# A two-layer decoder step: FFN statistics behind the last product, the mixer's sums and splits reordered, and samples finished on VectorE

## The reference, cut to what matters

```python
def layer(x, c, ...):
    mod = (silu(c) @ w_ada + b_ada).reshape(B, 9, D)
    s1, sc1, g1, s2, sc2, g2, s3, sc3, g3 = [mod[:, k] for k in range(9)]
    x = LN(ALPHA * x + 0.5 * (1 + g1) * swiglu(x * (1 + sc1) + s1), ln_g[0], ln_b[0])
    mix = mixer(x * (1 + sc2) + s2)          # pooling, RG-LRU, gate, @ w_out
    x = LN(ALPHA * x + (1 + g2) * mix, ln_g[1], ln_b[1])
    x = LN(ALPHA * x + 0.5 * (1 + g3) * swiglu(x * (1 + sc3) + s3), ln_g[2], ln_b[2])
```

## Time and profile before

| | |
|---|---|
| median of 3 runs | 998.52 us (998.02 to 999.37) |
| the profiled execution: its own time | 998.87 us |
| its span, first to last instruction | 997.1 us |
| mean granted TensorE clock | 0.997 |
| busy: PE, PEld | 978.1 us (98%), 932.2 us (93%) |
| busy: DVE, ACT, POOL | 611.8 us (61%), 450.6 us (45%), 103.6 us (10%) |
| PE product matmuls of lines 562 to 564 | x1648 each on `m`, x672 each on `h`; mean 283 to 287 ns |
| transfers | 235.67 MB, mean 236 GB/s |

### The profile page before, as it was taken

One profiled execution on the slowest core, in us unless ns is written; L12 is line 12 of the kernel. 1 busy time (PEld: TensorE's weight loads), 2 busy tenths in 40 slices (PEclk: granted clock), 3 DMA queues, 4 the chain that ended last, 5 costly groups with the idle time before them and its releaser, 6 DMA issues. The chain is left out here.

```text
span 997.1 us, 19778 instructions
## 1 busy us (share of the span) xinstructions
PE 978.1 (98%) x8598; PEld 932.2 (93%) x8598; DVE 611.8 (61%) x932; ACT 450.6 (45%) x546; POOL 103.6 (10%) x160
## 2 busy tenths in 40 slices
PE   6999999999999999999999999999999999999996
PEld 4999999998998999999989999999898899999996
DVE  2566454567898665554676655465689776555564
ACT  2354444235674545342345534343468554444340
POOL 1240000000310610000006000000030043000000
PEclk9999999999999999999999999999999999999998
DMA  9999888993749897959578796868563967664631
GB/s 335 321 253 334 275 260 297 317 333 122 295 138 306 289 261 196 313 181 318 181 229 240 196 326 189 298 212 295 170 244 106 330 168 212 190 188 154 227 112 44
DMA packets 259313, 235.67 MB, mean 236 GB/s; under 512 B 7647, under 2 KB 237145, under 8 KB 259210
## 3 DMA queue, kind: packets, MB, share of 16 engines
q1 hardware_dynamic: 256848, 230.71, 72.8%
q0 software_dynamic: 2080, 3.58, 1.2%
q10 hardware_dynamic: 298, 0.10, 0.0%
HBM read 233.11 MB, written 1.78 MB: 236 GB/s over the span
## 5 line engine op out<-in xcount | busy, mean ns | idle before, releaser
L562 PE MATMUL bank<-m_hi,w_hi 128*128 128x264 f32 x1648 | 470.7, 286 | 0.9 <-DVE m_lo L1206 0.5
L563 PE MATMUL bank<-m_lo,w_hi 128*128 128x264 f32 x1648 | 467.3, 284 | 0.0
L564 PE MATMUL bank<-m_hi,w_lo 128*128 128x264 f32 x1648 | 466.7, 283 | 0.0
L1134 DVE TENSOR_TENSOR w_lo<-raw,w_hi 128x2048 fp32r<-128x2048 f32 (+2 forms) x150 | 324.9, 2166 | 200.6 <-ACT w_hi L899 199.9
L899 ACT ACTIVATE w_hi<-raw 128x2048 fp32r<-128x2048 f32 (+2 forms) x149 | 266.8, 1792 | 173.9 <-PE bank L564 150.9
L562 PEld LDWEIGHTS bank<-m_hi,w_hi 128*128 128x128 f32 x1648 | 310.3, 188 | 7.8 <-issue 5.7
L563 PEld LDWEIGHTS bank<-m_lo,w_hi 128*128 128x128 f32 x1648 | 310.5, 188 | 0.1
L564 PEld LDWEIGHTS bank<-m_hi,w_lo 128*128 128x128 f32 x1648 | 309.3, 188 | 0.0
L562 PE MATMUL bank<-h_hi,w_hi 128*128 128x264 f32 x672 | 192.8, 287 | 0.0
L564 PE MATMUL bank<-h_hi,w_lo 128*128 128x264 f32 x672 | 190.9, 284 | 0.0
L563 PE MATMUL bank<-h_lo,w_hi 128*128 128x264 f32 x672 | 190.8, 284 | 0.0
(11 more groups left out here) (240 smaller groups left out, 560.3 us busy)
## 6 DMA issues: line engine op xcount, KB each, us to landing
raw<-in_ffn_wgu_dram SPq DMA_DIRECT2D x160, 512.0 KB, 5.2
ada_raw<-in_w_ada_dram SPq DMA_DIRECT2D x72, 1024.0 KB, 9.0
raw<-in_ffn_wdown_dram SPq DMA_DIRECT2D x48, 512.0 KB, 3.5
raw<-in_ffn_wdown_dram SPq DMA_DIRECT2D x48, 384.0 KB, 4.3
raw<-in_w_in_dram SPq DMA_DIRECT2D x24, 512.0 KB, 4.5
raw<-in_w_out_dram SPq DMA_DIRECT2D x16, 384.0 KB, 7.0
raw<-in_w_out_dram SPq DMA_DIRECT2D x8, 256.0 KB, 7.1
raw<-in_ffn_wgu_dram SPq DMA_DIRECT2D x2, 768.0 KB, 8.7
```

Source lines behind the costliest of these rows:

```text
L562: pe.matmul(out, hi, r_hi, start=start, stop=False)
L563: pe.matmul(out, hi, r_lo, start=False, stop=False)
L564: mm = pe.matmul(out, lo, r_hi, start=False, stop=stop)
L1134: dve.tensor_tensor(lo[:, 0:n], src[:, 0:n], hi[:, 0:n].bitcast(F32), ALU.subtract).then_inc(lo_split, 1)
```

## The change

- **FFN ends (three of the four).** The two statistics between output 6 and output 7 go. After output 7 PE sums `sqs[:, 0]`, `sqs[:, 6]`, `zsum`, `z[:, 7]`, `sqs[:, 7]`. `zsum` now holds tile 6 too: POOL adds it, in a new function `sum_seven`.
- **`variance`** multiplies the samples by their coefficient into `sq`, behind the first mean subtraction; `normalise` has one sample operation less there.
- **Mixer ends (both).** DVE takes tiles 2 to 5 one by one and adds each to `zsum`. PE sums `zsum`, tile 6 and tile 7. The coefficients come before the wait for the mean. The split of unit g0 + 6 comes after the mean's subtraction, ahead of `split_half` of g0 + 7; PE's wait for that half moves behind the first products.
- **Tail.** DVE does the samples' three steps and the transpose between the prompt's blocks; ACT stores one half of the samples and SP, behind the prompt's last block, the other.

```diff
+            def sum_seven(l, f):
+                n = l * 3 + 2 * f
+                pool.wait_ge(sums_ready, 2 * l + f + 1)
+                pool.wait_ge(evicted, n * DT + 7)
+                pool.tensor_tensor(zsum[:], zsum[:], z[:, 6], ALU.add).then_inc(seven_summed, 1)
...
             for l in range(DEPTH):
+                sum_seven(l, 0)
                 finish_x(l, 0)
...
                 if l + 1 < DEPTH:
+                    sum_seven(l, 1)
                     finish_x(l, 2)
...
-            samples = z[:, :, TP:T]
-            pool.wait_ge(samples_less_mean, 1)
-            pool.wait_ge(sample_rstd, 1)
-            pool.tensor_tensor(samples, samples, token_rstd[:, 2:2 + B].unsqueeze(1).broadcast_to([P, DT, B]), ALU.mult)\
...
                 for j in range(2):
+                    if f and j and k == 0:
+                        pe.wait_ge(half_split, l + 1)
...
                         for i in range(2):
-                            if pair == 3 and third == 2 and i == 1 and (l, f) != (DEPTH - 1, 1):
-                                pe.wait_ge(sums_ready, 2 * l + f + 1)
-                                stat(bank[MEAN], mean_w, zsum[:], True, False)
-                                stat(bank[VAR], mean_w, sqs[:, 0], True, False)
...
             def ffn_stats(l, f):
                 n, s = l * 3 + 2 * f, l * 15 + f * 10
-                pe.wait_ge(evicted, n * DT + 7)
-                stat(bank[MEAN], mean_w, z[:, 6], False, False)
+                pe.wait_ge(sums_ready, 2 * l + f + 1)
+                stat(bank[VAR], mean_w, sqs[:, 0], True, False)
                 pe.wait_ge(squared, s + 4)
                 stat(bank[VAR], mean_w, sqs[:, 6], False, False)
+                pe.wait_ge(seven_summed, 2 * l + f + 1)
+                stat(bank[MEAN], mean_w, zsum[:], True, False)
                 pe.wait_ge(evicted, n * DT + 8)
                 stat(bank[MEAN], mean_w, z[:, 7], False, True).then_inc(mean_out, 1)
...
             def mixer_stats(l):
                 n, s = l * 3 + 1, l * 15 + 5
-                pe.wait_ge(evicted, n * DT + 5)
+                pe.wait_ge(mixed_sum, l + 1)
                 stat(bank[MEAN], mean_w, zsum[:], True, False)
-                stat(bank[MEAN], mean_w, z[:, 4], False, False)
                 pe.wait_ge(evicted, n * DT + 7)
-                stat(bank[MEAN], mean_w, z[:, 5], False, False)
                 stat(bank[MEAN], mean_w, z[:, 6], False, False)
...
                 subtract_mean(0)
+                own.wait()
+                own.then(dve.tensor_tensor(sq[:, :, TP:T], z[:, :, TP:T], coef[:, 0, :, 1:C], ALU.mult))
...
-                split(g0 + 6)
-                residuals((2, 3))
-                dve.wait_ge(evicted, n * DT + 4)
-                for m in (2, 3):
-                    own.then(dve.tensor_tensor(zsum[:], zsum[:], z[:, m], ALU.add))
-                residuals((4,))
-                residuals((5, 6))
+                for m in range(2, 6):
+                    residuals((m,))
+                    dve.wait_ge(evicted, n * DT + m + 1)
+                    if m < 5:
+                        own.did(dve.tensor_tensor(zsum[:], zsum[:], z[:, m], ALU.add))
+                    else:
+                        dve.tensor_tensor(zsum[:], zsum[:], z[:, m], ALU.add).then_inc(mixed_sum, 1)
+                residuals((6,))
                 residuals((7,))
+                coefficients(l, 2)
                 dve.wait_ge(mean_out, n + 1)
                 dve.wait_ge(evicted, (n + 1) * DT)
                 for a, b in ((0, 1), (1, 2), (2, 4), (4, 6), (6, 8)):
                     dve.tensor_tensor(z[:, a:b], z[:, a:b], wide(bank[MEAN][:, 0:T], b - a), ALU.subtract)\
                        .then_inc(less_mean, b - a)
-                coefficients(l, 2)
+                split(g0 + 6)
                 split_half(g0 + 7, 0).then_inc(half_split, 1)
...
+            own.then(dve.tensor_tensor(samples, samples, weights, ALU.mult))
+            for i, (a, h) in enumerate(BLOCKS):
                 c = slice(h * HALF, (h + 1) * HALF)
                 dve.scalar_tensor_tensor(x_rows[:, a, c], x_rows[:, a, c], token_rstd[:, a:a + 1], bias_rows[:, c],
                                          ALU.mult, ALU.add).then_inc(y_ready, 1)
-            dve.wait_ge(sample_steps, 3)
-            dve.transpose(ys[:, 1], ys[:, 0]).then_inc(samples_turned, 1)
+                if i == 0:
+                    dve.wait_ge(sample_rstd, 1)
+                    own.did(dve.tensor_tensor(samples, samples, token_rstd[:, 2:2 + B].unsqueeze(1).broadcast_to([P, DT, B]),
+                                              ALU.mult))
+                elif i == 1:
+                    own.wait()
+                    own.did(dve.tensor_tensor(ys[:, 0].rearrange("p (b m) -> p m b", m=DT), samples, biases, ALU.add))
+                elif i == 2:
+                    own.wait()
+                    dve.transpose(ys[:, 1], ys[:, 0]).then_inc(samples_turned, 1)
```

More of the change, by code:

```diff
@@ L239, in trunk @@
         y_ready = sem("y_ready")
-        sample_steps = sem("sample_steps")
         consts = sem("consts")
@@ L314, in trunk @@
         trio_lo = sem("trio_lo")
+        mixed_sum = sem("mixed_sum")
+        seven_summed = sem("seven_summed")
         gu_view = [w.rearrange("l (k p) (h f c) -> l h f p k c", p=P, h=2, c=P) for w in (ffn1_wgu, ffn2_wgu)]
@@ L346, in trio_part, with store_samples @@
             return tile[:].rearrange("p s c -> p (s c)")[:, first + k0 * n:first + k1 * n]
+        def store_samples(eng, h):
+            eng.dma_start(y_sample[h * B // 2:(h + 1) * B // 2].rearrange("b o (m g j) -> g b (o m) j", g=4, j=32),
+                          ys[:, 1, 32 * h:32 * (h + 1)]).then_inc(y_stored, 16)
         block = ctx.enter_context(nc.Block())
@@ L422, in _ @@
                     .then_inc(y_stored, 16)
+            sync.wait_ge(samples_turned, 1)
+            store_samples(sync, 1)
             sync.wait_ge(y_stored, 6 * 16)
@@ L1111, in _ @@
             act.wait_ge(samples_turned, 1)
-            for h in range(2):
-                act.dma_start(y_sample[h * B // 2:(h + 1) * B // 2].rearrange("b o (m g j) -> g b (o m) j", g=4, j=32),
-                              ys[:, 1, 32 * h:32 * (h + 1)]).then_inc(y_stored, 16)
+            store_samples(act, 0)
         @block.vector
@@ L1261, in normalise @@
                 full(0)
-                own.then(dve.tensor_tensor(samples, z[:, :, TP:T], rstd[:, TP:T].unsqueeze(1).broadcast_to([P, DT, B]),
-                                           ALU.mult))
-                own.then(dve.tensor_tensor(samples, samples, coef[:, 0, :, 1:C], ALU.mult))
+                root = rstd[:, TP:T].unsqueeze(1).broadcast_to([P, DT, B])
+                if i == 1:
+                    own.then(dve.tensor_tensor(samples, z[:, :, TP:T], root, ALU.mult))
+                    own.then(dve.tensor_tensor(samples, samples, coef[:, 0, :, 1:C], ALU.mult))
+                else:
+                    own.then(dve.tensor_tensor(samples, samples, root, ALU.mult))
                 dve.tensor_tensor(samples, samples, coef[:, 1, :, 1:C], ALU.add).then_inc(sample_full, 1)
@@ L1623, in _ @@
             dve.wait_ge(mean_squared, 2 * DEPTH)
-            dve.tensor_tensor(z[:, :, TP:T], z[:, :, TP:T], bank[6][:, 0:B].unsqueeze(1).broadcast_to([P, DT, B]),
-                              ALU.subtract).then_inc(samples_less_mean, 1)
+            samples = z[:, :, TP:T]
+            weights, biases = (a.unsqueeze(2).broadcast_to([P, DT, B]) for a in (ln_g_of(DEPTH - 1, 2), ln_b_of(DEPTH - 1, 2)))
+            own.did(dve.tensor_tensor(samples, samples, bank[6][:, 0:B].unsqueeze(1).broadcast_to([P, DT, B]), ALU.subtract))
             dve.tensor_tensor(token_rstd[:, 2:2 + B], bank[7][:, 0:B], h_full[:, 0:B], ALU.subtract).then_inc(sample_var, 1)
```

3 lines of the change are left out of this document (removed).

## The result

The changed kernel takes 992.97 us (median of 6 runs, 992.31 to 994.17); the kernel before, in 6 runs beside them, 998.49 us (998.02 to 999.37). The medians are 5.5 us apart. The ratio is 0.995, with a 95% interval of 0.9939 to 0.9961, that is, 5.0 us faster, between 3.9 and 6.1. The forecast was 3.9 us, and the range began 0.7 us above what was measured. The profiled execution took 992.94 us with a span of 990.4, so the span is 6.6 us shorter. In the 36 runs of the changed kernel and of those built on it, it is 1.76 to 3.55, on average 2.41. So some 0.6 us of what the spans win doesn't reach the time. No part of the change shows this by itself, and no run shows what takes it.

The account below looks back on a forecast made before the run. PE was busy for 978.1 us, so time could be won by fewer matmuls, matmuls done during waits, or shorter waits. FFN ends 1.8, mixer ends 2.1 and tail 0 sum to 3.9 us: 998.52 to 994.6, range 993.7 to 996.8.

Parts of the forecast that it names:

- FFN end: Each of three FFN ends: 0.51 us from the last statistic coming sooner plus 0.08, together 0.59; 1.8 for three.
- the 0.08 is won too: FFN end: PE's wait of some 0.08 us for `m_lo`, ahead of the first product, goes.
- Mixer end: Each of two mixer ends: tile 7's statistic starts 1.07 us sooner; 2.1 for two.
- 1.33 a tile: Mixer end: DVE's time per tile in the new order, 0.59 + 0.21 + 0.44 + 0.09 us.
- DVE still binds: Mixer end: PE is done with tile 7 since 788.24, while DVE's last residual steps end at 789.92.
- The bound named for the mixer: Both mixer ends together: a gain from 0.1 to 2.3 us, with up to 1.0 lost if the split slid on.
- Splits behind the subtraction: Mixer end: splits of 2.2 and 1.1 us fit ahead of the first normalised tile, with 0.2 to spare.
- I take 0: Tail: last store done at 994.05 as before, so no gain; from -0.3 to +0.7 us.
- Nothing is left: Rival, chance 0.06: what comes sooner at the ends is waited for at a transfer later; 998.5 us.
- the two halves: Rivals: only the mixers gain, 996.4 us, chance 0.12; only the FFNs gain, 996.7 us, chance 0.10.
- POOL's longest row: Slower rival, chance 0.06: POOL's sum ends 2.06 us later, each FFN end loses about 1.5; 1000.8 us.
- The rule weighed: FFN end: GpSimd and two-SBUF-input VectorE operations exclude each other; tile 7's 8-column step would wait until 714.50.

Follow-up runs that it names:

- e9_sample_move: The kernel before with only the samples' coefficient multiplication moved into `variance`, behind the first mean subtraction; 1000.1 us in one run.
- e1_tail: The kernel before with the tail's part alone: samples on DVE between the blocks, stores split between ACT and SP; 997.3 us, ratio 0.9997.
- e4_pool_last: The whole change plus a one-column memset by POOL at the very end, which nothing waits for; 995.35 us, ratio 0.9971.
- e2_ffn: The kernel before with the FFN's part alone: two statistics moved, tile 6 summed by POOL, sample operation moved into `variance`; 997.6 us, ratio 0.9996.
- e3_mixer: The kernel before with the mixer's part alone: tiles summed one by one, three statistics instead of five, split behind the subtraction; 995.2 us, ratio 0.9971.
- e7_order_only: The kernel before with the mixer's part, but the split of unit g0 + 6 left between tiles (0, 1) and tile 2; 1001.6 us, ratio 1.0039.

## Why the prediction was right and wrong

The sign was right, but the forecast gain of 3.9 us is only the lower end of the measured interval, and the time was below the range. The terms show why.

- **FFN end, right to 0.13 us.** The order on PE, POOL's 0.74 for the 0.75 taken, its start 0.15 behind tile 6 and the hidden sum are as laid out. By terms: the two statistics gave 0.85 for 0.90 within the products (at layer 0's first end it is 31.79 us for 32.23 from the vector product before it to its own, and the length has grown by 0.41); those behind output 7 added 0.41 for 0.39 (the working's 715.03 should be 714.56 + 0.45 = 715.01, a slip of 0.02); the step that failed is "the 0.08 is won too": 0.02 was won (e9_sample_move). I took DVE's operations for the only chain that leads to `m_lo` and didn't ask when ACT's `m_hi` is there: it ended at 718.78 + 0.51 = 719.29 in the kernel before, and DVE's `m_lo` began at 719.44, so 0.15 us were there to win at most, less a semaphore:

```profile
718.78 0.51 ACT L957 ACTIVATE m_hi<-sq,coef 128x256 fp32r<-128x256 f32 x1 [0.62 <-DVE sq L1252]
...
719.44 0.48 DVE L1257 SCALAR_TENSOR_TENSOR m_lo<-sq,coef,m_hi 128x256 fp32r<-128x256 f32 x1
```

- **The moved sample operation** hides behind the mean's subtraction, as costed: DVE still waits 0.27 us for the root, where it waited 0.38.
- **Mixer end, the mechanism right, the size wrong.** Two steps failed. The first is "1.33 a tile": the distance is 1.26 (779.86 to 781.12 above), and ahead of tile 6 it is 0.35 from the addition to the next residual (783.64 to 783.99) instead of the 0.53 that I laid out (0.44 and 0.09), since DVE needn't wait for that addition; together 0.39 us (three tiles of 0.07, and 0.18). The second is that I started DVE's order where the trace had it. That execution had landings of 6.13 and 6.21; those of the changed kernel were 5.82 and 5.76, and gave DVE some 0.4 us more. With both, DVE is no longer late, and "DVE still binds" falls for this execution: PE's own 6.93 binds. At the landing of 6.21 that I had, the table's rule gives 7.27, so DVE would still have bound; I had forecast 7.75 (8.82 - 1.07). Of the 0.8 us missed at that mixer, 0.5 is the cost that I laid out too long and 0.3 the transfer's chance. I also read "DVE is late" without asking what ACT waited for: the transfer of unit g0 + 6, which the moved split takes off the path.
- **The bound named for the mixer** (up to 2.3 for two) was too narrow for the same reason: it asked only what could be lost behind the subtraction. If PE's own work had been laid out as a floor, its 6.93 would have shown that 1.9 was open.
- **Splits behind the subtraction, right.** 0.2 us to spare was forecast, 0.18 is there; the vector product hides the rest, since the product behind it starts at 3.59 everywhere.
- **Tail, wrong.** The path of the stores was right: the last issue, now SP's and before ACT's, ends 0.02 us earlier, counted from the first variance sum (7.34 for 7.36), and SP closes 11.67 us behind the last product for 11.62. But "I take 0" took the stores for the end. The last row of the profile and the end of the span are 3 us apart, and I never asked who fills these. POOL did, and it left the tail. That is 1.13 us, shown by e1_tail and e4_pool_last.
- **The rivals.** "Nothing is left" and the two halves are excluded, and POOL's longest row didn't come: all three sums are 0.74. The price of a late sum was right: 0.70 for 0.70.
- **The rule weighed.** By the Trainium skill, page "SBUF — State Buffer", section "SBUF: two separate sides", DVE's 8-column step would have started behind POOL's sum, at 711.34 or later. It started at 711.21, and 14 further ends in five kernels show the same. For a step this short the measurement speaks against the rule; for the long split of 2291 or 2911 ns no run here tells.

What the change gives on average can be put together from the stages: three FFN ends of 0.46, and the tail's 1.13. The eight mixers of the kernels with DVE's old order average 8.64 (four kernels) and the twelve of the kernels with the whole mixer part 7.07 (six), so 1.6 each. The sum is 1.4 + 3.2 + 1.1 = 5.7 us of the span, or some 5.1 of the time, if the 0.6 outside the span is taken off. The two comparisons gave 5.5 and 4.5 (medians), and their intervals reach from 3.0 to 6.1. The medians of the three parts alone (e1_tail 0.9, e2_ffn 0.6, e3_mixer 3.0) add up to 4.5.

## What to carry to other kernels

Lay out every engine's own path as a floor, also those that were early before: a gain goes on until the next one binds, and it can't be priced from the engine that is late now. If a path starts with a transfer, one profiled execution gives one landing; take the spread from as many like transfers as the trace has. At a kernel's end ask what lies between the last row and the end of the span, and don't let GpSimd have the last work there: in these kernels it closed 4.3 us behind it.

## What the runs showed of the hardware

**GpSimd closes late.** 4.32 to 4.34 us pass from the end of its last operation to its close, in the three kernels of the table, and a write of one column cost as much as the three operations of the samples (tails of 13.09 and 13.03 us).

**Landings spread.** The same 768 KB behind the same issue reached ACT after 5.32 to 6.91 us in 24 cases, at granted clocks of 0.995 to 0.998.

**The clock can fall in one wait.** In e7_order_only PE stood still for 1.87 us, from 788.88 to 790.75, until DVE's sum came (the row of L585 above). Stretches of that mixer end (columns as above):

```profile
786.40:788.80 2.40, 2.40 (x21) 2.27 (x19) 2.20 (x8) 1.90 (x2) 0.00 (x0) 1.00 1.03 410
788.80:791.20 2.40, 0.53 (x2) 0.44 (x2) 2.23 (x9) 0.00 (x0) 0.00 (x0) 0.92 1.03 410
791.20:793.60 2.40, 2.40 (x6) 1.30 (x4) 1.33 (x7) 0.00 (x0) 0.00 (x0) 0.50 1.03 410
```

PE was busy for 0.53 of 2.40 us, and then the granted clock was 0.50, the 1.2 GHz level, from 790.84 to 794.25, while PE did its statistics: two of `z` took 1.97 us, where the changed kernel takes 1.35 above. It is why this mixer takes 10.12 at the shortest landing but one: 5.45 + 3.82 would be 9.27. In layer 0 of the same kernel PE waited longer, 2.51 us, and the clock stayed at 1.00:

```profile
310.27 0.71 PE L585 MATMUL bank<-zsum,mean_w 128*128 128x264 f32 x2 [2.51 <-DVE zsum L1568]
310.94 1.39 PE L585 MATMUL bank<-z,mean_w 128*128 128x264 f32 x4
```

So the shorter wait cost the clock and the longer one didn't; the length of the wait alone doesn't decide it, and what does stays open.
